# S1 to S4 of the activations' blocks turned and summed by TensorE, in a four-layer streaming encoder trunk on one core

## The reference, cut to what matters

```python
def half_ffn(x, i, n):
    h = 0.5 * (silu(x @ ffn_w1[i, n]) * (x @ ffn_w3[i, n])) @ ffn_w2[i, n]
    return layer_norm(ALPHA * x + h, ln_g[i, 2 * n], ln_b[i, 2 * n])
for i in range(DEPTH):
    x = half_ffn(x, i, 0)
    m = pool_mixer(...) if i % 2 == 0 else stick_breaking(...)
    x = layer_norm(ALPHA * x + m, ln_g[i, 1], ln_b[i, 1])
    x = half_ffn(x, i, 1)
    gate, e = sigmoid(x @ ple_w_gate[i] + ple_b_gate[i]), p[i] @ ple_w_proj[i]
    x = layer_norm(ALPHA * x + gate * e, ln_g[i, 3], ln_b[i, 3])
```

## Time and profile before

| | before |
|---|---|
| median of three runs | 2495.22 us (2495.19 to 2495.64) |
| profiled execution: time, span | 2500.3 us, 2498.6 us |
| PE busy | 2427.4 us, 97% of the span |
| DVE, ACT, POOL busy | 1660.6, 1102.9, 470.5 us (66%, 44%, 19%) |
| chain that ended last | PE 86%, DVE 7%, ACT 3%, issue 3%, DMA 1% |
| mean granted PE clock | 0.99 |

### The profile page before, as it was taken

One profiled execution on the slowest core, in us unless ns is written; L12 is line 12 of the kernel. 1 busy time (PEld: TensorE's weight loads), 2 busy tenths in 40 slices (PEclk: granted clock), 3 DMA queues, 4 the chain that ended last, 5 costly groups with the idle time before them and its releaser, 6 DMA issues.

```text
span 2498.6 us, 38673 instructions
## 1 busy us (share of the span) xinstructions
PE 2427.4 (97%) x15358; PEld 2174.5 (87%) x15358; DVE 1660.6 (66%) x2166; ACT 1102.9 (44%) x1769; POOL 470.5 (19%) x399
## 2 busy tenths in 40 slices
PE   7999999989999999899999999999999999999998
PEld 7999999879999998799999988777776799999986
DVE  5866666877666676776666662666666776666667
ACT  4433343344333343543344333666665443344343
POOL 4211123222211110311121101122123321111100
PEclk9999999999999999999999999999999999999999
DMA  4322222223222223132222225777876132322231
GB/s 132 94 79 85 85 85 93 60 73 98 75 85 85 85 94 94 41 95 85 85 85 85 84 77 148 207 194 206 230 203 182 45 109 80 95 85 73 82 102 68
DMA packets 376642, 259.14 MB, mean 104 GB/s; under 512 B 10321, under 2 KB 339025, under 8 KB 376464
## 3 DMA queue, kind: packets, MB, share of 16 engines
q1 hardware_dynamic: 371360, 239.64, 33.3%
q0 software_dynamic: 5104, 17.04, 2.1%
HBM read 248.22 MB, written 8.42 MB: 103 GB/s over the span
## 4 chain that ended last, share of the span: by engine, by line
PE 86%; DVE 7%; ACT 3%; issue 3%; DMA 1%; POOL 0%; SPq 0%; DVEq 0%; ACTq 0%
PE ps L2496 77%; PE ps L797 5%; PE ps L829 2%; DVE ring L1884 1%; DVE x L1956 1%; DVE x L1942 1%; DVE small L1902 1%; PE ps L905 0%; ACT ring L1373 0%; DMA raw<-in_ffn_w_dram 0%; PE ps L2545 0%; PE ps L2602 0%; ACT e_buf L1582 0%; ACT xt_hi L1391 0%; POOL t_buf L1151 0%
## 5 line engine op out<-in xcount | busy, mean ns | idle before, releaser
L2496 PE MATMUL ps<-xt_hi,ring 128*128 128x320 f32 (+2 forms) x3328 | 791.2, 313 | 22.3 <-DVE tmp L2052 8.7
L2496 PEld LDWEIGHTS ps<-xt_hi,ring 128*128 128x128 f32 x3328 | 576.7, 191 | 35.1 <-DVE tmp L2052 9.6
L2496 PE MATMUL ps<-ring,h_hi 128*128 128x512 f32 x1760 | 556.7, 392 | 8.5 <-DVE x L1942 4.6
L1884 DVE TENSOR_TENSOR ring<-raw,ring 128x1024 fp32r<-128x1024 f32 (+1 forms) x318 | 437.2, 1378 | 129.3 <-ACT ring L1373 129.1
L2496 PE MATMUL ps<-xt_lo,ring 128*128 128x320 f32 (+2 forms) x1664 | 518.8, 312 | 0.0
L2496 PE MATMUL ps<-s_ops,ring 128*128 128x320 f32 x3168 | 510.5, 311 | 7.7 <-DVE s_ops L2015 7.7
L2496 PEld LDWEIGHTS ps<-s_ops,ring 128*128 128x128 f32 x3168 | 479.5, 189 | 8.7 <-DVE s_ops L2015 8.7
L2496 PEld LDWEIGHTS ps<-ring,h_hi 128*128 128x128 f32 x1760 | 331.5, 188 | 82.8 <-DVE x L1942 6.3
L1373 ACT ACTIVATE ring<-raw 128x1024 fp32r<-128x1024 f32 (+1 forms) x318 | 287.3, 931 | 238.0 <-PE ps L2496 211.8
L1151 POOL TENSOR_TENSOR t_buf<-raw,t_buf 128x512 f32<-128x512 f32 x88 | 115.9, 1317 | 1346.0 <-DVE t_buf L1897 1346.0
L2496 PE MATMUL ps<-ring,h_lo 128*128 128x512 f32 x880 | 344.0, 391 | 0.0
(11 more groups left out here) (188 smaller groups left out, 2505.4 us busy)
## 6 DMA issues: line engine op xcount, KB each, us to landing
raw<-in_ffn_w_dram SPq DMA_DIRECT2D x264, 512.0 KB, 4.1
k_raw<-in_cache_k_dram SPq DMA_DIRECT2D x128, 256.0 KB, 5.0
v_raw<-in_cache_v_dram SPq DMA_DIRECT2D x128, 256.0 KB, 4.3
raw<-in_sb_w_in_dram SPq DMA_DIRECT2D x24, 512.0 KB, 5.5
raw<-in_ple_w_gate_dram SPq DMA_DIRECT2D x16, 512.0 KB, 3.9
g_b<-in_ln_g_dram POOLq DMA_DIRECT2D x8, 512.0 KB, 5.6
b_b<-in_ln_b_dram POOLq DMA_DIRECT2D x8, 512.0 KB, 7.1
raw<-in_sb_w_out_dram SPq DMA_DIRECT2D x8, 512.0 KB, 5.8
```

Of the source, the lines that this page charges most:

```text
L1884: ve.tensor_tensor(ring[:, slot, 1, col:col + cols], conversion_source(u), ring[:, slot, 0, col:col + cols].bitcast(F32), ALU.subtract).th ...
L2496: return pe.matmul(out, w, xx, start=first, stop=last, skip_group_check=True)
```

## The change

1. `pair_sums`, `pair_sums12` and `pair_sums43` go (instructions of 128x512, 4 on POOL and 4 on DVE for each of the four ffns, 32 in all). DVE gets two differences of whole tiles per ffn, `left_diffs` (x0 - x2) and `right_diffs` (x1 - x3).
2. PE makes the sums as it turns: S12 is 16 accumulated transposes and 2 matmuls with the negative identity (S1 minus X11's rounded part and rest) where it was 8 transposes; S43 is 12 where it was 8.
3. Not after the load, S12a's rest is made by PE (`subtract_sums12`) and ACT (`low_sums12`). In embed the x pieces' rests go from PE and ACT to DVE.
4. Banks and order: S43a now comes right behind S12a, P2(2) stands before P5(0), S43b between P5(0) and P6(0).
5. DVE: `first_diffs(1)` now stands behind `low_sums43(b)`. At the stage's end `gate_of_first(0)` stands between `centre` and `rescale` of the last tile; in pool `spread(2)` and `normalise(2)` stand before `first_diffs(next, 0)` and the residual sum `mix(3)`.
6. ACT: B(0) is rounded and `first_product(0)` read before the last `deviation`. Item B(0) comes before C(0), except after the load.

```diff
 # plan_items, st.prev.kind != "load"
+                gate(2)
+                first_diffs(0)
+                up(0)
 # ACT, block_products, not after the load
+                    hi_sums12(prev, 0)
+                    first_product(st, 1)
+                    low_sums12(prev, 0)
+                    hi_sums43(prev, 0)
+                    hi_sums12(prev, 1)
+                    cvt_to(unit["C", 0] + 1)
+                    silu_of_first(st, 0)
 # ACT, ends of out and pool (embed alike)
+                    cvt_to(unit["B", 0] + 1)
+                    first_product(st.next, 0)
                     deviation(st, 4)
 # DVE
+            def left_diffs(st):
+                ve.tensor_tensor(pair_diff[:, 0, :], x[:, 0, :], x[:, 2, :], ALU.subtract).then_inc(diff_a, 1)
 # DVE, block_products, after the load
+                    left_diffs(prev)
+                    right_diffs(prev)
                     gate_of_first(st, 0)
+                    low_sums12(prev, 0)
+                    cvt_to(unit["B", 0] + 1)
+                    low_sums43(prev, 0)
+                    gate_of_first(st, 1)
+                    low_sums12(prev, 1)
+                    cvt_to(unit["A", 2] + 1)
 # DVE, otherwise
+                    cvt_to(unit["B", 0] + 1)
+                    gate_of_first(st, 1)
+                    cvt_to(unit["C", 0] + 1)
+                    low_sums43(prev, 0)
+                    low_sums12(prev, 1)
+                    right_diffs(prev)
                 cvt_to(unit["D", 0] + 1)
+                low_sums43(prev, 1)
                 first_diffs(st, 1)
-                low_sums43(prev, 1)
+                hidden_of_first(st, 0)
                 cvt_to(unit["B", 1] + 1)
-                hidden_of_first(st, 0)
 # DVE, end of embed
+                        if t in (2, 3):
+                            low(st, t - 2)
                         if t == 3:
                             add_bias(TILES + t + 1)
+                            low(st, 2)
                             centre(st, t)
 # DVE, pool
                     mix(2)
+                    spread(2)
+                    normalise(st, 2)
                     first_diffs(st.next, 0)
                     mix(3)
-                    spread(2)
-                    normalise(st, 2)
 # PE
+            def turn_sum(bank, first, second):
+                for block in (first, second):
+                    for c in range(HC if block is not None else 0):
+                        ins = turned(ps[:, bank, c * P:(c + 1) * P], block[:, c * P:(c + 1) * P], block is first and c == 0)
+            def turn_sums12(st, b):
+                turn_sum(bank, x[:, 2 + b, 0:HK], x[:, 2 + b, HK:])
+                turn_sum(bank + 1, x[:, 2 + b, 0:HK], x[:, 2 + b, HK:])
+                for xx in (xt_hi, xt_lo):
+                    ins = mm(ps[:, bank + 1, :].rearrange("p (c t) -> p c t", t=P), neg_ident[:],
+                             xx[:, 0:HC, pair_columns(b)], False, True)
+            def turn_sums43(st, b):
+                turn_sum(bank, pair_diff[:, b, 0:HK], None)
+                turn_sum(bank + 1, pair_diff[:, b, 0:HK], pair_diff[:, b, HK:]).then_inc(piece_full, 1)
                     turn_sums12(prev, 0)
+                    turn_sums43(prev, 0)
+                    if prev.kind != "load":
+                        subtract_sums12(prev, 0)
                     product2(st, 1)
                     turn_sums12(prev, 1)
-                    turn_sums43(prev, 0)
                     if prev.kind == "load":
                         product1(st, 2)
+                    product2(st, 2)
                     product5(st, 0)
+                    turn_sums43(prev, 1)
                     product6(st, 0)
```

## The result

The changed kernel takes **2519.09 us** (median of four runs, 2516.99 to 2519.45), and the kernel before 2495.43 (2495.19 to 2499.37); of its four runs three are those of the first measurement, and the one run since took 2499.37. The ratio is 1.0089, 95% interval 1.0072 to 1.0107: 0.9% slower, clear of the noise, and 2.6 us above the range. The forecast was 2508.0. The sign, the place and most mechanisms came as forecast, the size did not.

What follows compares the result with a forecast made beforehand. PE, never idle inside an ffn, bounds the kernel, so only the four ffn starts change: load +3.9, pool +6.2, embed -1.0, out +3.7, together +12.8 us on the runs' median, giving 2508.0 us; range 2499.5 to 2516.5.

Steps and rivals of the forecast that it cites:

- The bound, and PE's prices: PE never idle inside an ffn, so only starts change; 0.10 us a turn, 3.3 to 3.8 us more PE work each.
- The pause before P5(0): PE waits 3.1 us behind P2(2) for ACT's and DVE's queue of C(0) and rests; P5(0) at T + 19.4.
- the pause before P1(2): After the load, P1(2) waits 3.7 us for A(2), whose rest on DVE is behind S12b's rounding and rests.
- The load of up 2: In each start first_diffs(2) waits for this load, issued later; P5(2) 17.9 us behind P3(0), 14.9 without the load.
- the load of up 2 is in time: Rival: the load lands within 3.4 us or its slot frees 3 us earlier; 3.0 us saved per start, 2496.0; chance 0.10.
- P1(0) after pool: Second ffn's first matmul comes 7.0 us later, near 510, as first_diffs(0) now follows normalise(2)'s wait for the root.
- pool's start is not held back: Rival: the root of tile 2 comes before 495, so pool's start is not late; 2501 us, chance 0.09.
- both: Rival: up 2 lands in time and pool's start is not held back; 2489 us, faster, chance 0.07.
- P1(0) after embed and out: T comes 4.65 us earlier after embed, rests now on DVE, and 0.4 earlier after out, where a subtraction no longer waits.
- The sum of the spans: Change per start: load +3.9, pool +6.2, embed -1.0, out +3.7; together +12.8 us.
- the clock term after pool: Slow clock charged in pool's start: 0.5 us for the pause before P5(0), 0.85 for what precedes T.
- the base: Runs' median, 5.1 us below the 2500.3 us profile, got the same 12.8 us: 2508.0; the profile would be 2513.1.

Runs made afterwards that it cites:

- a_rows_later: Kernel after, with POOL issuing the loads of the gain and bias rows behind diffs(3) instead of diffs(1): 2505.77 us, ratio to before 1.0032.
- a_diffs1_first: Kernel after, with first_diffs(1) again before low_sums43(b) on DVE: 2504.47 us, ratio to before 1.0030.
- b_pool_order: Kernel before, with spread(2) and normalise(2) moved before first_diffs(next, 0) and mix(3) in pool: 2506.06 us, ratio to before 1.0025.
- best_order: Kernel after, with pool's order restored, first_diffs(1) before low_sums43(b), C(0) between S43a's and S12b's steps, A(2) earlier after the load: 2480.65 us, ratio 0.9928.
- a_pool_order: Kernel after, with first_diffs(next, 0) and mix(3) again before spread(2) and normalise(2) in pool: 2508.76 us, ratio to before 1.0045.
- best_dve_sums2: best_order with left sums again by POOL, right sums by DVE, PE turning finished sums, S12a's rest kept: 2487.97 us, ratio to before 0.9957.
- a_turns_more: Kernel after, with the eight turns of the first bank of S12a and of S12b made twice: 2524.04 us, 5.0 above the kernel after.

## Why the prediction was right or wrong, point by point

**The bound, and PE's prices: right.** Inside the ffn nothing moved, and all shifts arose before P5(2). Turns cost 0.104 to 0.108 us (0.10 taken, limit 0.13). S12a took 2.27 us (2.05) and S43a 1.34 (1.2) after embed. With both S12 and the longer first products, T to P5(0) without a slow stretch was 20.21 and 20.14 instead of 19.4.

**The pause before P5(0): right as a wait, wrong as a cost.** 2.99 us for 3.1, from the queue described; after the load the pause before P1(2) was 3.63 for 3.7. That it was avoidable the prediction didn't need; but its slow stretch is the larger error (below).

**The load of up 2: right.** P3(0) to P5(2) 17.6 to 18.05 us for 17.9, in all four starts, with the DMA named as releaser and 6.2 to 6.7 us to land. a_rows_later and a_diffs1_first showed both halves of the reason. Undone, 14.3 us stay, not 14.9. The rival "the load of up 2 is in time" fell.

**P1(0) after pool: right.** 7.3 us for 7.0, and b_pool_order has 7.3 with nothing else changed. The rival "pool's start is not held back" fell, and with it "both".

**P1(0) after embed and out: right.** It came 10.07 us later after embed, where the last stage's arrival (the first turn of the stage's end, 1025.54 for 1010.48) was 15.06 later: -5.0 (-4.65 forecast). After out -0.66 (-0.4).

**The sum of the spans.** By start, forecast and measured: load +3.9 and +5.8; pool +6.2 and +10.0; embed -1.0 and -1.3; out +3.7 and +4.9. They make 19.4; the stages between took back 0.9 (1.3 of it before pool, where a slow stretch lies at 440 to 451 us in before and at 480 to 488 in after; elsewhere 0.4 were added), in all +18.5 for +12.8.

**Step that failed, one: the clock term after pool.** I charged 0.5 us for the pause before P5(0) and 0.85 for what precedes T. The stretches of the kernel after that hold P1(0) to P2(0) and P5(0) with S43b, columns as the earlier trace rows:

```profile
514.67:524.10 9.43, 9.43 (x48) 9.43 (x49) 8.32 (x12) 4.04 (x6) 0.00 (x0) 0.73 0.00 0
537.10:541.70 4.60, 4.59 (x25) 4.58 (x25) 2.22 (x2) 0.00 (x0) 0.00 (x0) 0.66 0.20 59
```

The first cost 2.4 us (9.43 for 7.04) and the second 1.4 (P5(0) and S43b took 4.51 us, 3.11 in best_order), together 3.8 for 1.35 charged. The prediction itself moved P1(0) by 7 us, which on PE made a pause of 8.09 us out of one of 1.23, and yet priced what follows as if the old pauses stood there. In a_pool_order, with the short pause back, the same products took 7.14 us. That is 2.5 of the pool start's 3.8 us of error; about 0.7 are the longer S12, S43a and first products, 0.3 T and 0.3 the way from P5(0) to P3(0). After out the longer first stretch is 0.7 of the 1.2. After embed it was covered: 2.55 was charged for the clock, and about 1.5 came. The load's 1.9 is 0.85 of a later T (15.67 for 14.82, with PE's pauses before it 1.96 and 4.44 us; it lay between 14.4 and 15.9 in the profiles), 0.6 the longer S12 and S43a, and the rest small differences on the way to P3(0). The clock term is the size of the profile that was measured: by the 15 starts with the pause of 2.99 us, the part behind it can as well be nothing or 2.7 us.

**Step that failed, two: the base.** I put 12.8 us on the lowest known level of the kernel before, the median of three runs within 0.5 us, 5.1 below its own profile. In 76 later runs that kernel lay between 2493.6 and 2501.5, with medians of 2496.8 to 2500.2: the three runs lay near the low end of a spread, and the profile was not an outlier. The changed kernel's profile (2518.89, where 2513.1 was forecast) lies at its median (2519.09). Against 2498 to 2500 it is 19 to 21 us slower, which fits the spans; against 2495.4 it is 23.7. So 5 of the 11 us of error are this step, and the other 6 the clock and S12. What puts a run at one end is not fully settled: the two profiles show slow stretches that come and go in the first 22 us, but they are two.

**What I had not asked.** The prediction took the order as one piece with the sums. The experiments part them. Three places in the lists (the root before first_diffs, C(0) before the rests, first_diffs(1) behind S43b's rest) cost 27.7 us together. With them and A(2) repaired, the kernel is 17 us under the kernel before, of which the sums on PE are 5.6 to 7.3 and some 12 are there without them: best_dve_sums2 lies 12.2 us under the runs beside it. How much of the 12 the kernel before would gain from reordering alone was not run.

## What to carry to other kernels

When work is moved between engines, price the new queue on every engine line by line, then test the cheapest reordering before judging the move: here the kernel with the sums on PE was 21 us slower or 17 faster than before by its order of work. A pause on TensorE of 2 to 3 us costs itself and often a slow stretch behind it (3.7 us for 2.25 of pause; a slow stretch in eleven of 15), and when a step makes a pause longer, the clock behind it must be priced anew; two such costs at one place overlap rather than add. A base of three equal runs is no base: set a difference of profiles on the level of the profiles, and widen the range by the distance between profile and median.

## What the runs showed of the hardware that I had not expected

- A 512 KB load landed in 6.6 us when two 512 KB broadcasts of a row were issued at that moment, and in 3.9 when they came later, at the same place of the program.
- Fp32 turns that accumulate cost what plain ones cost (16 in 1.67 us to the next instruction), and follow the clock: 8 in 1.03 us at full, 1.97 at half.
- Pauses of 0.74 us before P5(0) were followed by a full clock in every start read; pauses of 2.99 by a low one in eleven starts of 15, and by a full one after pool in a_pool_order, after embed and out in a_rows_later and after out in a_turns_more. The stretch from 440 to 451 us had a clock of 0.69 in both profiles of before and of 1.00 in that of after.
- POOL's step of 128x512 took between 1.28 and 2.24 us and DVE's between 0.68 and 1.63; the long ones shown above stand where both engines read their operands from SBUF at once.
